# A two-layer hybrid decoder step on one core: streamed expert blocks chosen on chip by key length, ids decoded in 16-bit elements, down products spread over the samples' slots

## The reference

```python
q = (xf @ w_q).reshape(n, PEER_HEADS, 2, PEER_QHALF)          # 8 heads, 2 halves of 64
s = einsum('nhcd,hckd->nhck', q, keys)                        # 128 keys for each half
s1, i1 = top_k(s[:, :, 0], 16)
s2, i2 = top_k(s[:, :, 1], 16)
cand = s1[..., :, None] + s2[..., None, :]                    # 256 candidates a head
cidx = i1[..., :, None] * 128 + i2[..., None, :]
top, sel = top_k(cand, 16)
eidx = take_along_axis(cidx, sel)                             # 16 experts a head, of 16,384
gate = softmax(top)
...
hid = gelu(einsum('nkd,nd->nk', U[eb], xb))                   # 128 experts a token
out = einsum('nk,nkd->nd', hid * gb, V[eb])                   # U, V: 16384 x 1024
```

## Time and profile before

| | us |
|---|---|
| median of 3 runs | 2248.09 (2241.82 to 2250.54) |
| profiled execution, its own time | 2249.12 |
| its span, first to last instruction | 2247.0 |
| TensorE busy (matmuls) | 2040.1 (91%) |
| VectorE busy | 1434.2 (64%) |
| ScalarE busy | 829.3 (37%) |
| GpSimd busy | 757.3 (34%) |
| mean granted clock of TensorE | 0.969 |

### The profile page before, as it was taken

How to read it: one execution, slowest core, us unless ns; L and a number is a source line. 1 busy time by engine, 2 the same in 40 slices (tenths; PEclk the granted TensorE clock), 3 DMA queues, 4 the chain that set the end, 5 groups by cost and what they waited for, 6 DMA issues and landing times. The chain is left out here.

```text
span 2247.0 us, 37166 instructions
## 1 busy us (share of the span) xinstructions
PE 2040.1 (91%) x13044; PEld 1251.5 (56%) x13044; DVE 1434.2 (64%) x3297; ACT 829.3 (37%) x2404; POOL 757.3 (34%) x658
## 2 busy tenths in 40 slices
PE   7998979999999778999989898899999998789996
PEld 5777668774444222555477776787644442235553
DVE  1425454579998898544623354644899989974445
ACT  1221222034445775333422213220444467733333
POOL 0400000025555666544403000000455456655452
PEclk9999989999999999999999999999999999999998
DMA  6330233669999999999953201436799999999996
GB/s 260 121 114 2 79 107 128 221 223 363 353 388 396 371 388 377 376 376 397 355 216 113 95 5 76 160 131 240 262 345 366 390 382 363 365 359 394 377 368 241
DMA packets 120676, 597.91 MB, mean 266 GB/s; under 512 B 38635, under 2 KB 40587, under 8 KB 57227
## 3 DMA queue, kind: packets, MB, share of 16 engines
q0 software_dynamic: 76032, 417.87, 48.4%
q1 hardware_dynamic: 42784, 174.46, 21.3%
q10 hardware_dynamic: 1696, 3.45, 0.4%
HBM read 724.97 MB, written 6.58 MB: 326 GB/s over the span
## 5 line engine op out<-in xcount | busy, mean ns | idle before, releaser
L1451 POOL DMA_INDIRECT arena<-in_uv,arena x264 | 339.8, 1287 | 293.8 <-PE ps L962 249.6
L1451 POOL DMA_INDIRECT ring<-in_uv,arena x264 | 331.7, 1256 | 265.1 <-PE ps L962 213.1
L1971 DVE SCALAR_TENSOR_TENSOR arena<-ring,arena 128x1024 bf16<-128x1024 f32 x264 | 320.1, 1224 | 138.6 <-DMA ring<-in_uv,arena 124.1
L1971 DVE SCALAR_TENSOR_TENSOR arena<-arena 128x1024 bf16<-128x1024 f32 x264 | 320.2, 1224 | 124.5 <-DMA arena<-in_uv,arena 108.6
L962 PE MATMUL ps<-arena 64*64 64x512 f32 x2112 | 293.5, 627 | 61.1 <-ACT arena L1343 55.3
L962 PE MATMUL ps<-ring,arena 64*64 64x512 f32 x2112 | 289.1, 622 | 38.9 <-ACT arena L1343 35.7
L1341 ACT ACTIVATE arena<-arena 128x1 f32<-128x1 f32 x528 | 106.4, 202 | 581.6 <-DVE arena L1971 577.5
L1441 POOL COPY arena<-arena 128x8 uint32 (+1 forms) x66 | 35.5, 538 | 742.9 <-DVEq L1942 742.5
L1040 PEld LDWEIGHTS ps<-hold,ub 128*128 128x128 f32 x1024 | 182.6, 191 | 150.0 <-issue 131.4
L1040 PE MATMUL ps<-hold,ub 128*128 128x256 f32 x1024 | 265.4, 397 | 0.0
L632 PE MATMUL ps<-xn,ring 128*128 128x264 f32 x1024 | 244.0, 397 | 14.0 <-remote 12.3
(11 more groups left out here) (429 smaller groups left out, 2380.9 us busy)
## 6 DMA issues: line engine op xcount, KB each, us to landing
ring<-in_w SPq DMA_DIRECT2D x88, 1024.0 KB
ub<-in_uv SPq DMA_DIRECT2D x64, 512.0 KB
ub<-in_ud SPq DMA_DIRECT2D x48, 512.0 KB
hold<-in_ud SPq DMA_DIRECT2D x16, 512.0 KB, 8.8
ring<-in_uv,arena POOLq DMA_INDIRECT x264
arena<-in_uv,arena POOLq DMA_INDIRECT x264
hold<-in_st SPq DMA_DIRECT2D x2, 2048.0 KB
out_st<-hold SPq DMA_DIRECT2D x2, 2048.0 KB
```

Of the source, the lines that this page charges most:

```text
L1451: e.indirect_dma_start(out=row(k), out_offset=None, in_=A["uv"], in_offset=bass.IndirectOffsetOnAxis(ap=ix[:, par, k:k + 1], axis=0), **sk ...
L1971: stt(prod[:, n % 2, :], u, 1.0, xtok[:, tt, :], ALU.mult, ALU.mult, accum_out=hid[:, k:k + 1]).then_inc(S("dve_hid"), 1)
```

## The change

Four things change.

1. *Which first keys are streamed.* They were the last 32 of 128. Now the sum of squares of each first key over all heads is computed on chip at the start of a layer, taken through DRAM so that every partition has all 128, and VectorE picks the 32 largest (`picked`). SyncE loads the numbers of the blocks from there into registers (`pick`) when it issues their transfers, and `ud` holds all 128 blocks of U. Being streamed is no longer a comparison with `FIRST_DENSE`: `member` compares the 16 first-half keys of each head with the 32 picked ones and adds 128 to a key that is one.
2. *Decoding.* The two positions of a candidate (`ja`, `jb`) used to be cast, compared, multiplied and summed one after the other in float32. Now ScalarE spreads both out at once as bfloat16 (`jx`), and VectorE compares and multiplies both in one 16-bit pass each, and sums by halving. The shift of the softmax's exponent is in ScalarE's bias.
3. *Places.* `numerators` stands at the slot after the fourth piece, since the spread positions are needed by the fifth.
4. *The end of a layer.* The 256 down products are spread over 88 slots, the samples' eight with them. `add_down` and the squares stand in the last 8 slots, and `sum_squares_first` behind the last of them.

```diff
@@ SyncE
                 for n in range(4):
                     block_of(n % 4, l * N_BLOCKS + n)
+                e.dma_start(first_keys, lay("first_keys").rearrange("a p c -> p (a c)")).then_inc(S("sp_keys"), 16)
...
+                e.wait_ge(S("dve_pick"), 1)
+                e.dma_start(O["scratch_n"][:, :], key_norm).then_inc(S("sp_keys"), 16)
+                e.wait_ge(S("sp_keys"), 32)
+                e.dma_start(norms, O["scratch_n"].rearrange("c b -> b c").to_broadcast([P, P])).then_inc(S("sp_keys"), 16)
                 for n in range(4, 20):
                     block_of(n % 4, l * N_BLOCKS + n)
...
+                def pick(j):
+                    return e.value_load(picked[0:1, j:j + 1], min_val=0, max_val=P - 1)
+
                 for m, j in enumerate(AHEAD):
-                    e.dma_start(ahead[:, m, :], A["ud"][bass.ds(l * DENSE + j, 1)].rearrange("a p c -> p (a c)")).then_inc(S("sp_hold"), 16)
+                    e.dma_start(ahead[:, m, :], A["ud"][bass.ds(pick(j) + l * P, 1)].rearrange("a p c -> p (a c)")).then_inc(S("sp_hold"), 16)
@@ TensorE
-                    n = SAMPLES_AT * SLOT + P - DOWN_AT
+                    n = SAMPLES_AT * SLOT + P - DOWN_AT + SLOT
                     for s in range(n):
-                        weighted(s % SLOT, 1)
+                        if s == n - SLOT:
+                            e.wait_ge(S("dve_xa"), 1)
+                            open_sum(0, 1)
+                        weighted(s % SLOT, 1 if s < n - SLOT else 2)
...
                 for k in range(SLOT):
                     weighted(k, 1)
-                    if k == 0:
+                    if k == 7:
                         sum_squares_first(l)
@@ ScalarE
                     e.wait_ge(S("dve_top"), n)
-                    act(t16[0:p1, 0:nh, :], t16[0:p1, 0:nh, :], ACT.Exp).then_inc(S("act_top"), 1)
+                    k = 2 * nh * TOPK
+                    act(jx[0:p1, 0:k * TOPK].rearrange("p (a b) -> p a b", b=TOPK), bc(jj[0:p1, 0:k], 2, [p1, k, TOPK]), ACT.Copy).then_inc(S("act_top"), 1)
+                    own(act(tneg[0:p1, 0:nh], t16[0:p1, 0:nh, 0], ACT.Copy, scale=-1.0))
+                    for h in range(nh):
+                        i = act(t16[0:p1, h, :], t16[0:p1, h, :], ACT.Exp, bias=tneg[0:p1, h:h + 1])
+                    i.then_inc(S("act_top"), 1)
@@ VectorE, at the start of a layer
+                stt(ub[:, 2, 0:PH * HD], first_keys, 1.0, first_keys, ALU.mult, ALU.mult, accum_out=key_norm).then_inc(S("dve_pick"), 1)
+                e.wait_ge(S("sp_keys"), 48)
+                left = norms
+                for n in range(DENSE // 8):
+                    own(e.max(norms_top[:, 8 * n:8 * n + 8], left))
+                    own(e.max_index(picked[:, 8 * n:8 * n + 8], norms_top[:, 8 * n:8 * n + 8], left))
+                    if n < DENSE // 8 - 1:
+                        own(e.match_replace(norms_left[n % 2], norms_top[:, 8 * n:8 * n + 8], left, -BIG))
+                        left = norms_left[n % 2]
@@ VectorE, cand_first
+                            own(tt_(member.rearrange("p (j a) -> p j a", a=w), bc(i1, 1, [P, DENSE, w]), picked_t.rearrange("p (j a) -> p j a", a=w), ALU.is_equal))
+                            own(tt_(member[:, 0:16 * w], member[:, 0:16 * w], member[:, 16 * w:32 * w], ALU.add))
...
+                            own(tt_(member[:, 0:w], member[:, 0:w], member[:, w:2 * w], ALU.add))
+                            own(stt(i1, member[:, 0:w], float(P), i1, ALU.mult, ALU.add))
@@ VectorE, decode
+                        e.wait_ge(S("act_top"), 2 * n - 1)
+                        own(tt_(oh_, jx_, bc(iota16[0:p1, :], 1, [p1, k, TOPK]), ALU.is_equal))
+                        o4 = oh_.rearrange("p (q j) a -> p q j a", j=TOPK)
+                        own(tt_(o4, o4, bc(ixb.rearrange("p s h a -> p (s h) a"), 2, [p1, 2 * nh, TOPK, TOPK]), ALU.mult))
```

More of the change, by code:

```diff
@@ L203, in build @@
         small = sb("small", [P, 32])
+        picked = sb("picked", [P, DENSE], U32)
+        picked_f = sb("picked_f", [P, DENSE])
         arena = sb("arena", [P, ARENA])
@@ L214, in build @@
         ahead = hold[:, :].rearrange("p (a b) -> p a b", b=D)
+        first_keys, key_norm = ub[:, 0, 0:PH * HD], ub[:, 0, PH * HD:PH * HD + 1]
+        norms, norms_left = ub[:, 1, 0:P], [ub[:, 1, P + P * i:2 * P + P * i] for i in range(2)]
+        norms_top = ub[:, 1, 3 * P:3 * P + DENSE]
         def C(name, n=None):
@@ L1380, in _ @@
                 e.wait_ge(S("sp_out"), 5 * 16)
-                ends = {ROUTE_FROM + ROUTE_EVERY * (r - 2) + PIECES[-1]: r + 1 for r in range(2, 2 * GROUPS)} | {SECOND_AT[-1]: 2}
+                ends = {ROUTE_FROM + ROUTE_EVERY * (r - 2) + PIECES[3] + 1: r + 1 for r in range(2, 2 * GROUPS)} | {SECOND_AT[0] + 1: 2}
                 samples = SAMPLES_AT * SLOT + P
@@ L1861, in _ @@
                 e.sem_inc(S("dve_qz"), 1)
+                own(e.tensor_copy(iota16, C("iota", TOPK)))
+                own(e.tensor_copy(picked_t.rearrange("p (j a) -> p j a", j=DENSE), bc(picked_f[:, :], 2, [P, DENSE, GH * TOPK])))
                 def first8(lists, src, tmp, val, idx):
@@ L1937, in finish @@
+                    def finish():
+                        own(tt_(oh_[:, :, 0:8], oh_[:, :, 0:8], oh_[:, :, 8:16], ALU.add))
+                        own(tt_(oh_[:, :, 0:4], oh_[:, :, 0:4], oh_[:, :, 4:8], ALU.add))
+                        own(e.tensor_reduce(e12[0:p1, 0:k], oh_[:, :, 0:4], AX_X, ALU.add))
+                        own(stt(n1, n1, 128.0, n2, ALU.mult, ALU.add))
                         if n == ROUTED_SAMPLES:
-                            own(ts(to_idx.bitcast(U32), flat(e1), layer_off[0:p1, 0:1], None, ALU.add))
+                            own(ts(to_idx.bitcast(U32), n1, layer_off[0:p1, 0:1], None, ALU.add))
@@ L1939, in finish @@
                         else:
-                            own(ts(flat(e2), flat(e1), float(FIRST_DENSE), float(SKIP), ALU.is_ge, ALU.mult))
-                            own(stt(to_idx.bitcast(U32), flat(e1), layer_off[0:p1, 0:1], flat(e2), ALU.add, ALU.add))
+                            own(ts(n2, n1, float(EXPERTS), float(SKIP), ALU.is_ge, ALU.mult))
+                            own(stt(to_idx.bitcast(U32), n1, layer_off[0:p1, 0:1], n2, ALU.add, ALU.add))
                             e.sem_inc(S("dve_route"), 1)
-                        e.wait_ge(S("act_top"), n)
+                        e.wait_ge(S("act_top"), 2 * n)
@@ L1947, in finish, with cand_positions @@
                         if n != ROUTED_SAMPLES:
-                            own(stt(gathered, flat(e2), 0.0, to_gate, ALU.is_equal, ALU.mult))
+                            own(stt(gathered, n2, 0.0, to_gate, ALU.is_equal, ALU.mult))
                         if n == ROUTED_SAMPLES:
                             e.sem_inc(S("dve_route"), 1)
-                    return keys_first, keys_second, cand_first, cand_second, weigh, finish
+                    def cand_positions():
+                        cand_second()
+                        positions()
+                    return keys_first, keys_second, cand_first, cand_positions, decode, finish
                 def group_routing(tt, g):
@@ L2043, in _ @@
                             dot(k, 2, s + k, row_round + s // SLOT)
-                            if k >= 3 and k < 7:
-                                add_down(k - 3)
                         row_round += 1
+                    if s >= samples + 2 and s < samples + 6:
+                        add_down(s - samples - 2)
+                    if s == samples + 6:
                         tt_(sqs[:, :, 0:P], x[:, :, 0:P], x[:, :, 0:P], ALU.mult).then_inc(S("dve_sq"), 1)
```

98 lines of the change are left out of this document (48 added, 50 removed).

## The result

| | before | after |
|---|---|---|
| median, us (10 executions each) | 2246.45 (2241.82 to 2256.53) | 2236.76 (2228.19 to 2243.47) |
| profiled execution, its own time | 2249.12 | 2228.19 |
| its mean granted clock | 0.969 | 0.978 |

The ratio is 0.9946, with a 95% interval from 0.9928 to 0.9965: 12 us faster by the ratio, 10 by the medians. The profiled execution of after is the fastest of its ten, and the one with the highest clock. The ten go in order of that clock: 2243.47 us at 0.964, 2240.0 at 0.971, 2233.49 and 2236.3 at 0.974, 2228.19 at 0.978. A line through them gives 12 us for 0.01 of mean clock, a line through 35 executions of before 10 us. So the 21 us between the two profiled executions are not the change's: at 0.009 of clock some 10 of them are luck, and stages have to be compared rather than spans.

The account below looks back on a forecast made before the run. Fewer bytes were taken to pay only where VectorE waits for rows (slots 0 to 167), with TensorE bounding slots 168 to 247. +10.6 + 6.6 - 25.7 - 2.0 = -10.5, taken as -9.5: 2239.6, said as 2240 us; range 2222 to 2268.

Parts of the forecast that it names:

- A and B: Each layer's expert slots 0 to 95 (up products beside them) and 96 to 167 (one-hots); together forecast at -19.1 us.
- Start, +10.6: Before each layer's first dot: ids wait behind ScalarE's copy, so the first dot comes 5.3 us later, twice.
- 16-bit passes: Decoding on VectorE: 0.69 us per 1,024-element pass, the lower bound; 4.7 us a group, 0.2 less than now.
- the rival on the slower side: Decoding's 16-bit passes run at one element per cycle: 18.7 us a layer more, 2277 in all; chance 0.12.
- Stage A, +6.6: Slots 0 to 95: VectorE waits 1.0 us per group for ScalarE's copy; +3.3 us a layer.
- the rival in which ScalarE starves TensorE: Slots 0 to 95: ScalarE, away 4.5 us instead of 2.8, delays TensorE; +12 us a layer, 2264 at most; chance 0.15.
- sign of being wrong: Slots 0 to 95: TensorE idle over 12 us was listed among the observations that would show the forecast wrong.
- Waits gone, -25.7, with 0 in C: Fewer gathered rows shorten VectorE's waits in slots 0 to 167 by 25.7 us; slots 168 to 247 (C) gain 0.
- End, -2.0: Each layer's end: down products over 88 slots give -4.4 us, the longer tail +3.4; net -1.0 a layer.
- Picking the keys, 0: Near each layer's start: DRAM round trip and 13 picks hide under eight column tiles; uncovered, up to 7 us a layer.
- waits are not bandwidth: Rival for VectorE's row waits: they are latency behind late buffers, fewer bytes don't shorten them; 2264 us; chance 0.08.
- the transfers bind everywhere: Rival for all expert slots, 168 to 247 too: 77 us gone, near 2186 us; chance 0.02.

## Why the prediction held, term by term

The total was forecast as -9.5 and measured as -9.7 by the medians (-12 by the ratio). Two of its five terms were off and made up for each other, so that the close total is in good part luck. By stage, both layers together, the forecast was +10.6 for the start, -19.1 for A and B and -2.0 for C and the end; the traces show +10.8, -10.3 and -12.6.

- *Start, +10.6.* +5.4 a layer, so +10.8: the mechanism (the ids behind ScalarE's copy of the last tile) and the size were right. The run with the earlier copy shows it from the other side, -6.0 a layer on the start. The sum had 7.4 us for the ids (7.2), and 1.16 for the copy (1.06).
- *16-bit passes.* 0.69 us for 1,024 elements, 0.42 for 512, 0.29 for 256, 0.42 for the reduction of 256: the lower bound, and so the rival on the slower side is out. The rule that I set beside it (the Trainium skill, VectorE: DVE Perf Modes, "The perf-mode tier table (the rule you actually need)") agrees with these rows, also in that the reduction gained nothing: 256 bfloat16 elements took 0.42 us, as 256 float32 ones in a two-input pass did.
- *Stage A, +6.6.* With the old rows A is 240.4 and 237.4 against 234.2 and 236.5: +7.2 over both layers, near the forecast as a sum, though it was 6.2 and 0.9 where 3.3 each was forecast. The wait was 0.78 us instead of 1.0, seven times a layer. Fewer rows took 7.9 of it back, so that A ends where it was. Of the rival in which ScalarE starves TensorE a trace is seen (TensorE's waits in A of layer 0 went from 7.6 us in 12 to 13.9 in 9, which is over the 12 us that I had set as a sign of being wrong), but A as a whole is no longer than before, so that sign was set badly.
- *Waits gone, -25.7, with 0 in C.* This is the step that failed. A and B gave 18.4 together, not 25.7, because B stays 4 to 5 us above the 145 us that it takes without any rows; B was forecast at 145 and 148 and came out at 149.3 and 149.9. (The sum had even more: 155.6 - 12.7 is 142.9, below that floor.) And C, for which the prediction said "in C it is 0: TensorE hides it", gave 14.3. TensorE's 204.9 of 205.8 us showed that TensorE was full in the old order, and no more; there fewer rows did give its down products only 1.2 and 1.0 us. It did not show that the rows would come fast enough once its order was better. The old rows don't (the new end alone: no gain); fewer rows do.
- *End, -2.0.* Alone on the old kernel about +3, in the changed one -5.6 us by the medians, of which 2 at equal clock. So the term's own arithmetic, 88 slots of 2.47 us (measured 217 us from the first weighted product at 876.6 to 1094.4: 2.47 each), was right, but only on top of fewer rows. The tail was 15.3 us instead of the 18.2 that I had: an addition with its dot takes 1.87 us, and the 2.49 of the earlier trace rows was a cadence with 0.7 us of waiting in it. Not foreseen at all was the clock, which doesn't fall in the samples' slots any more.
- *Picking the keys, 0.* In layer 1 the round trip ended at 1144.69, the picks took 4.3 us, and VectorE then waited 6.6 us more for ScalarE; TensorE's first ten column tiles ran unbroken from 1120.35 on (37.38 us; 38.47 before). From the closing product of layer 0 to the last query tile of layer 1 it is 462.0 us, 461.5 before. No cost is seen; no run left the picking out.

The rival "waits are not bandwidth" is refuted by the runs with old rows and with the shortest keys, and "the transfers bind everywhere" by the run without rows: with no rows at all A and C are less than 2 us a layer shorter than in after.

## What to carry to other kernels

Two resources that are both full in a stage hide each other's worth: an engine without a gap says that relieving the other alone gives little (here 1 us a layer in TensorE's stretch), not that relieving both gives only the first one's share. Measure the stage on the engine that is full: the dots, which run ahead of it, showed 5.6 and 7.6 us where it had gained 1.2 and 1.0. So price such a pair of edits together, and test the four corners. And when a helper engine's result moves from behind an urgent step to in front of it, look for the earliest slot in the helper's queue: moving one copy past two tiles gave back 7 us of the 11 that the new order had cost.

## What the runs showed of the hardware

- A DMA share of 0.98 or 0.99 was not the ceiling: it meant 373 to 381 GB/s in the kernel before, while 1.00 came with 387 and 400 GB/s. The last 2% of the share held up to 5% of the rate, and equal shares of 1.00 came with rates 3% apart.
- Pauses of 1.4 us between products of 1.1 us were followed by the lower clock at every layer's end in both profiles with the old end (0.88 and 0.89 in before, 0.89 and 0.89 in the changed kernel); where TensorE went through unbroken it was 1.00 in after. With the new end on the old rows, where it went through too, it was 0.96 and 1.00.
- The mean granted clock goes with the spread between executions of one kernel: 0.964 to 0.978 in after went with 2243 to 2228 us, and a line through its ten leaves little. In the kernel before the line leaves half of the spread, and the six executions with the decoding one slot later show no slope at all.
